# Layer 0 heads of a two-layer encoder kernel: attention weights turned by DMA transposes instead of on TensorE

## The reference, cut to what matters

```python
def stick_breaking_attention(q, k, v):      # strictly causal
        z = einsum(q, k) * scale
        log_stay = where(mask, log_sigmoid(-z), 0.0)
        after = cumsum(log_stay, reverse=True) - log_stay
        w = where(mask, exp(log_sigmoid(z) + after), 0.0)
        return einsum('bhqs,bshd->bqhd', w, vf)

def forgetting_attention(q, k, v, f_logit):  # causal
        logits = einsum(q, k) * scale + cq - cum_k
        p = softmax(where(mask, logits, -inf))
        return einsum('bhqs,bshd->bqhd', p, vf)
```

## Time and profile before

| | us |
|---|---|
| median of 3 runs (2885.72 to 2887.35) | 2886.86 |
| span of the profiled execution, first to last instruction | 2882.5 |
| sb pairs, from the first sb mask matmul to the first fox one | 240.9 (53.8 to 294.7) |
| fox pairs, to the end of the last pair's slots (about 521) | 226.3 |

### The profile page before, as it was taken

The page is one execution under the profiler, slowest core; times in us unless marked ns, Lnnn a source line. Parts: engine busy times, 40 slices in busy tenths (PEclk is TensorE's granted clock), DMA queues, the critical chain, the costliest instruction groups (busy, mean ns, idle before and its releaser), DMA issues.

```text
span 2882.5 us, 44624 instructions
## 1 busy us (share of the span) xinstructions
PE 2773.1 (96%) x16630; PEld 1456.3 (51%) x16912; DVE 1876.8 (65%) x2733; ACT 1081.0 (38%) x1765; POOL 1653.8 (57%) x918
## 2 busy tenths in 40 slices
PE   8999998899999999998899999999999999999998
PEld 4566665454444444444444444677764444444443
DVE  6777666486666674256999999677756756665042
ACT  4556555343333310014554333666653433332000
POOL 4777545336666669845347777600003566665884
PEclk9999999999999999999999999999999999999999
DMA  4222222431111143222113222211113211113322
GB/s 147 60 59 63 71 56 48 161 118 59 59 59 59 66 171 129 102 73 79 52 37 146 102 93 82 74 59 44 58 63 120 88 52 59 59 59 117 135 101 101
DMA packets 102990, 240.57 MB, mean 83 GB/s; under 512 B 42448, under 2 KB 42576, under 8 KB 102848
## 3 DMA queue, kind: packets, MB, share of 16 engines
q1 hardware_dynamic: 56352, 204.13, 19.9%
q10 hardware_dynamic: 46496, 34.48, 4.6%
HBM read 185.31 MB, written 31.51 MB: 75 GB/s over the span
## 4 chain that ended last, share of the span: by engine, by line
PE 85%; DVE 4%; ACT 3%; issue 3%; POOL 2%; ACTq 1%; DMA 0%; POOLq 0%; DVEq 0%
PE ps L1503 23%; PE ps L317 20%; PE ps L306 13%; PE ps L2310 6%; PE ps L584 5%; PE ps L341 3%; PE ps L2346 2%; PE ps L590 2%; PE ps L694 2%; PE ps L1830 2%; PE ps L779 2%; PE ps L756 2%; PE ps L2325 1%; PE ps L1874 1%; DVE pt_lo L715 1%
## 5 line engine op out<-in xcount | busy, mean ns | idle before, releaser
L262 POOL TENSOR_TENSOR w_hi<-w_stage,ones 128x1024 bf16<-128x1024 f32 (+1 forms) x115 | 235.1, 2044 | 137.9 <-PE ps L317 85.2
L265 POOL TENSOR_TENSOR w_lo<-w_stage,w_hi 128x1024 bf16<-128x1024 f32 (+1 forms) x115 | 262.6, 2283 | 9.0
L1320 DVE SCALAR_TENSOR_TENSOR x_res<-x_res,ps 128x1024 f32<-128x1024 f32 x32 | 39.0, 1218 | 338.1 <-PE ps L317 337.2
L317 PE MATMUL ps<-w_hi,hid_hi 128*128 128x512 bf16 x689 | 206.2, 379 | 1.6 <-POOL w_lo L265 0.8
L317 PE MATMUL ps<-w_lo,hid_hi 128*128 128x512 bf16 x690 | 206.4, 379 | 0.7
L317 PE MATMUL ps<-w_hi,hid_lo 128*128 128x512 bf16 x690 | 206.3, 379 | 0.7
L2310 PE MATMUL ps<-lat_hi,q_now 128*128 128x512 bf16 (+3 forms) x730 | 185.9, 323 | 1.2
L306 PE MATMUL ps<-xt_hi,w_hi 128*128 128x512 bf16 x598 | 179.2, 380 | 3.1 <-DVE score L1989 2.5
L306 PE MATMUL ps<-xt_hi,w_lo 128*128 128x512 bf16 x596 | 178.6, 380 | 0.8 <-issue 0.2
L306 PE MATMUL ps<-xt_lo,w_hi 128*128 128x512 bf16 x592 | 178.2, 381 | 0.8
L1503 PE MATMUL ps<-xt_lo,w_hi 128*128 128x512 bf16 x426 | 161.5, 379 | 0.5
(11 more groups left out here) (295 smaller groups left out, 7873.1 us busy)
## 6 DMA issues: line engine op xcount, KB each, us to landing
w_stage<-in_l_up SPq DMA_DIRECT2D x88, 512.0 KB, 3.2
w_stage<-in_l_down SPq DMA_DIRECT2D x88, 512.0 KB, 3.2
w_stage<-in_l_o SPq DMA_DIRECT2D x32, 512.0 KB, 4.7
w_stage<-in_l_q SPq DMA_DIRECT2D x32, 512.0 KB, 5.2
q_split<-q_out SPq DMA_DIRECT2D x32, 512.0 KB, 2.6
q_now<-q_split SPq DMA_DIRECT2D x16, 1024.0 KB, 4.8
w_stage<-in_l_qkv SPq DMA_DIRECT2D x24, 512.0 KB, 3.3
x_spilled<-x_res ACTq DMA_DIRECT2D x16, 512.0 KB, 2.6
```

Of the source, the lines that this page charges most:

```text
L262: pool.tensor_tensor(w_hi[slot][:, 0:cols], w_stage[slot][:, 0:cols], ones[:, 0:1].to_broadcast([P, cols]), ALU.mult).then_inc(w_cast[slot ...
L265: pool.tensor_tensor(w_lo[slot][:, 0:cols], w_stage[slot][:, 0:cols], w_hi[slot][:, 0:cols], ALU.subtract).then_inc(w_split[slot], 1)
L317: mm = pe.matmul(ps[:, bank + h, :], a[:, k, rows], w[slot][:, h * HALF:(h + 1) * HALF], start=(k == 0 and m == 0), stop=(k == tiles - 1 a ...
```

## The change

The transposes leave TensorE. ACT now writes the high half in the order in which the weights already lie (queries on partitions), SBUF to SBUF, one instruction for a step; DVE writes the low half in the same way. SP then issues a DMA transpose of the high half as soon as ACT has written it, and another of the low half when DVE has. Both halves are written in slot t+3 (`HI_AFTER = 0`), one slot earlier than before, so the values' matmuls keep their slots. PE waits for all eight transfers of a group before its first matmul. The `split` buffers share their bytes with `prob`, so what waited for PE's transposes (the fox exponentials, the sb scan) now waits for both transfers to land. POOL's result goes to `take` instead of `prob`; the setting of edge columns to zero ahead of the pairs goes away. SP's weight loads are written out between the transposes.

```diff
+        def weights_hi(act, kind, pair, t):
+            src, hi, _ = split_views(t)
...
+            act.activation(hi, src, ACT.Copy).then_inc(s_whi, 1)
+
+        def weights_lo(dve, pair, t):
+            src, hi, lo = split_views(t)
+            dve.wait_ge(s_whi, STEPS * pair + t + 1)
+            dve.tensor_tensor(lo, src, hi, ALU.subtract).then_inc(s_wlo0, 1)
+
+        def weights_turn(sp, pair, t):
+
+            m, g, qs = query_block(t) + 1, t % 8 // 4, query_block(t) % 4 * P
+            for part, (ready, done) in enumerate(((s_whi, s_turn_hi), (s_wlo0, s_turn))):
+                sp.wait_ge(ready, STEPS * pair + t + 1)
+                if t % 4 == 0 and part == 0:
+                    wait_if(sp, s_pv, 4 * pair + t // 4 - 1)
+                sp.dma_start_transpose(turned[g][:, 0:m, part, qs:qs + P],
+                                       split[t % 4][:, part, 0:m * P]).then_inc(done[t % 4], 16)
...
-                        pe.wait_ge(turning.lo, BATCHES * p + batches_through(4 * group + 3))
+                        for b in range(4):
+                            pe.wait_ge(s_turn_hi[b], turned_through(p, 4 * group + b))
+                            pe.wait_ge(s_turn[b], turned_through(p, 4 * group + b))
...
-                if kind_then == "sb":
-                    turning.turn(pe, p, t, s_wsb, STEPS * p + t + 1)
-                elif kind_then == "fox":
-                    turning.turn(pe, p, t, s_wfox, STEPS * (p - N_SB // 2) + t + 1)
...
-                    act.wait_ge(turning.made, turning.prob_free(pair, t))
+                    act.wait_ge(s_turn_hi[t % 4], turned_through(pair, t) - 16)
+                    act.wait_ge(s_turn[t % 4], turned_through(pair, t) - 16)
...
-                    wait_if(dve, turning.made, turning.prob_free(p1, t1))
+                    wait_if(dve, s_turn_hi[t1 % 4], turned_through(p1, t1) - 16)
+                    wait_if(dve, s_turn[t1 % 4], turned_through(p1, t1) - 16)
...
-            load_rest(sp, feed_qkv)
-            load_first(sp, feed_o0)
+            for n, pair in ((0, 1), (1, 1), (2, 1), (0, 2), (1, 2)):
+                load_piece(sp, feed_qkv, n, pair)
+            ahead = {4: (2, 2), 8: (0, 3), 13: (1, 3)}
+            for pair in range(N_PAIRS):
+                for t in range(STEPS):
+                    weights_turn(sp, pair, t)
```

More of the change, by code:

```diff
@@ L63 @@
 TURN_LAG = {"sb": 3, "fox": 3}
+HI_AFTER = 0
 assert SEQ % P == 0 and D_FF % P == 0 and N_DSA == 2 * N_PAIRS
@@ L524, in program, with weight_buffer @@
         stay = [low(f"stay{b}", [P, SEQ], F32) for b in range(2)]
-        prob = [low(f"prob{b}", [P, SEQ], F32) for b in range(2)]
+        def weight_buffer(place, b):
+            pair = sb(f"split{b}", [P, 2, SEQ], BF16, place.at)
+            return place(f"prob{b}", [P, SEQ], F32), pair
+        weights = [weight_buffer(low, b) for b in range(2)]
         assert low.at <= arena
@@ L529, in program @@
         mix_lo = room("mix_lo", [P, KT, SEQ], BF16)
-        prob += [room(f"prob{b}", [P, SEQ], F32) for b in range(2, 4)]
+        weights += [weight_buffer(room, b) for b in range(2, 4)]
+        prob, split = [w[0] for w in weights], [w[1] for w in weights]
         take += [room(f"take{b}", [P, SEQ], F32) for b in range(2, 4)]
@@ L674, in group_end @@
             return t % 8 // 4 if t % 4 == 3 else None
[L676 to L720, removed]
@@ L723, in program, with turned_through, split_views @@
-        turning = Turning("att0", prob, pt_hi, pt_lo, s_pv)
+        def turned_through(pair, t):
+            return 16 * (4 * pair + t // 4 + 1)
+        def split_views(t):
+            n = (query_block(t) + 1) * P
+            return take[t % 4][:, 0:n], split[t % 4][:, 0, 0:n], split[t % 4][:, 1, 0:n]
+        def weights_hi(act, kind, pair, t):
+            src, hi, _ = split_views(t)
+            if kind == "sb":
+                act.wait_ge(s_wsb, STEPS * pair + t + 1)
+            else:
+                act.wait_ge(s_wfox, STEPS * (pair - N_SB // 2) + t + 1)
+            act.activation(hi, src, ACT.Copy).then_inc(s_whi, 1)
@@ L777, in pair_tensor @@
                         ends = j == (TB, TB // 2)[g] - 1
-                        for m, pt in enumerate((pt_hi, pt_lo)):
-                            mm = pe.matmul(ps[:, 7, qs:512], v_both[hh][:, j, :], pt[g][:, j, qs:512],
+                        for m in range(2):
+                            mm = pe.matmul(ps[:, 7, qs:512], v_both[hh][:, j, :], turned[g][:, j, m, qs:512],
                                            start=(j == 0 and m == 0), stop=(ends and m == 1), skip_group_check=True)
@@ L992, in heads_sync @@
         def heads_sync(sp):
-            load_rest(sp, feed_qkv)
-            load_first(sp, feed_o0)
+            for n, pair in ((0, 1), (1, 1), (2, 1), (0, 2), (1, 2)):
[4 more added lines that the diff above has]
+                    weights_turn(sp, pair, t)
+                    n, further = ahead.get(t, (0, N_PAIRS))
+                    if pair + further < N_PAIRS:
+                        load_piece(sp, feed_qkv, n, pair + further)
+                    if (pair, t) == (N_PAIRS - 2, 8):
+                        load_piece(sp, feed_o0, 2, 0)
+                if pair == N_PAIRS - 3:
+                    for n in (3, 0, 1):
+                        load_piece(sp, feed_o0, n, 0)
         def heads_gpsimd(pool):
@@ L1057, in heads_vector @@
                 proj_evac_lo(dve, e, 0)
-            for b in range(4):
-                dve.memset(prob[b][:, P - 1:SEQ:P], 0.0).then_inc(s_edge, 1)
-            dve.wait_ge(s_edge, 4)
             all_pairs(dve, pair_vector)
```

35 lines of the change are left out of this document (18 added, 17 removed).

## The result

| | before, us | after, us |
|---|---|---|
| median of 4 runs | 2886.29 (2884.92 to 2887.35) | 2940.84 (2939.14 to 2944.53) |
| ratio, 95% interval | | 1.0186 [1.0172, 1.0201] |
| span of the profiled execution | 2882.5 | 2937.0 |
| sb part | 240.9 | 271.3 |
| fox part | 222.6 | 242.4 |

What follows compares the result with a forecast made beforehand. PE, busy 96% of the span, was taken to bound the kernel. Gains of 34 us (sb pairs) and 15 us (fox pairs) made 49 us off the 2882.5 us span: 2834, plus 4.4 for the median, 2838 us; range 2800 to 2920.

Steps and rivals of the forecast that it cites:

- the low half's price in "What the vector and scalar engines do now": Sb pairs: low half with both operands in SBUF takes 55 us instead of 47.9, bringing DVE to 189.6 us.
- Rival 4: Nothing much moves: DVE's SBUF reads meet POOL's, D about 5; kernel within 6 us of now; chance 0.07.
- Sb pairs, 207 us: Sb pairs: DVE's floor of 189.6 us plus 17.5 us gives 207 us, a gain of 34 us.
- a floor plus 17.5 us for uneven slots: Sb pairs: the bounding engine's idle time before, 17.5 us, was kept and added to DVE's floor of 189.6 us.
- The fox loop: Fox pairs: exponentials wait for transfers to land; two slots take 2.6 us + D, 6.6 us, so 211 us, gaining 15.
- D: Fox pairs: time from the low half's end to its landing, bounded by 2.4 to 5.6 us, taken as 4.0.
- rival 1: Fox pairs: short landings, D 3 us or less, gain 81 us, kernel 2806 us; chance 0.61 together with the forecast.
- SP's issue, 0.62 us: SP: 32 transposes and 3 loads a pair at 0.62 us each, 22 us a pair, hidden in 52.
- The queue: DMA queue: a pair's transposes at 31.6 ns a row take 36 us of some 52 us, so there is room.
- Rival 3: The DMA queue becomes the bound if transfers don't overlap: 86 us a pair, kernel 3111 us; chance 0.12.
- The removed transposes and the clock: Heads phase: removing 576 PE transposes cuts PE's busy time by 88.7 us; no clock change was forecast.
- Rival 2: Fox pairs: the loop decides with D above 5.6 us, slower, 2902 us at D = 6; chance 0.20.

Runs made afterwards that it cites:

- e6: Kernel before, PE's transposes kept, with the low half's float32 operand read from an SBUF constant instead of PSUM: 2978.9 us, ratio 1.0313.
- e9: Changed kernel with the low half's float32 operand read from unused PSUM banks: 2906.8 us, ratio 1.0069.
- e5: Changed kernel with POOL's splits of the coming pairs' weights cut to 16 columns: 2914.2 us, ratio 1.0094.
- e11: e8 with the low half's float32 operand read from PSUM: 2890.0 us, ratio 1.0008 to the kernel before.
- e1: Changed kernel with four buffers for the fox exponentials that share no bytes with `split`: 2933.4 us, ratio 1.0149.
- e12: e11 with both halves, the value matmuls and all that follows them a slot later: 2896.8 us, ratio 1.0024.
- e4: Changed kernel with only the high half's transposes issued, read by both matmuls: 2915.9 us, ratio 1.0090.
- e7: Changed kernel with plain DMA copies of the same rows in place of the transposes: 2929.7 us, ratio 1.0144.
- e8: e1 with one DMA transpose a step for both halves, 128 instructions: 2922.4 us, ratio 1.0114.
- e3: Changed kernel with DVE's low half cut to 16 columns: 2909.5 us, ratio 1.0068.

## Why the prediction was wrong, point by point

**The step that failed: the low half's price in "What the vector and scalar engines do now".** I took the row of 1.526 us for 1024 columns as the price of the form, 55 us, and kept scan and product as they were. It measured 80.5 us, and the scans, which the prediction left as they were, went from 108.2 to 122.4 (the same window's row of the kernel before for L896 has 108.22), and DVE's sum is 227.4 us, not 189.6. It isn't the form that costs more: low halves of 1024 columns took 1195 ns in the mean in the sb pairs, less than the 1526 of the row. At that price 288 blocks would be an estimated 43 us, so some 37 of the 80.5 are waiting. The cause is shown from four sides: the operand put into SBUF in the kernel before (e6), taken out of it in the changed one (e9), POOL's splits shortened (e5), and the timeline. Rival 4 names it ("its reads of SBUF meet POOL's"), with at most 6 us for the kernel, where it is 27.5 in the sb part alone.

The Trainium skill has the rule, and I left it out: SBUF — State Buffer, section "SBUF: two separate sides", says that a VectorE operation with two SBUF inputs and a GpSimd operation that reads SBUF take the same port as an exclusive lock, and that whichever starts second stands still until the first is through. The traces agree: the 640-column low half ended 0.68 us after POOL's split, the scans 2.1 ns a column after POOL's products, and 16 columns took 510 ns in the mean. The low half before the change read only one of its inputs from SBUF, and by the rule that leaves it alone: none took longer than 693 ns.

**Sb pairs, 207 us.** Measured 271.3. With the operand's cost taken away it is 244, so the larger part of this miss, 37 of 64 us, lies in a second step: a floor plus 17.5 us for uneven slots. PE's floor of 180.6 was itself too low (200.4 us busy in e11, at a clock of 0.96), and to the busiest engine there came 43.7 us of idle time and not 17.5. PE had 43 us less to do, and none of it showed. PE's waits moved to DVE's low halves of the projections, which share one PSUM bank (in e11 20.1 us for `nq_lo` and 10.6 for `nv_lo`, where the sb part before had 1.2 and none), and the copy in slot t+3 waits for POOL. Putting it later trades that for the landing. Which of these holds the 244 stays open: buffers of their own for the sb weights as well, which would tell the ring from the landing, weren't tried.

**The fox loop.** The wait was there (70.5 us of it), but it didn't set the pace. The landing was 2.9 us in the median, and up to 7.9. It is counted from the start of the issue: one low half ended at 346.38 us, its issue started at 346.4 and landed 2.9 us later, and the exponentials that waited for it started at 349.40. So the median D is that of rival 1 and not the 4.0 of the forecast, and the loop with it, 2.6 + 2.9 us for two slots, would give 176 us for the fox pairs: a gain, where there was a loss. Taking the wait out gave 8.1 us (e1). What together made 24.2 us (242.4 to 218.2) is the wait (8.1), SP's issues (2.3) and the SBUF operand (13.8) by the parts, in this order of removal; the totals of the same runs fell by 7.4, 11.0 and 32.4 us (the last with the sb part in it), so only the first of the three and their sum are firm. The forecast of 211 us to the end of the slots, some 207 as the fox part is counted here, wasn't reached even with all three gone and the copy a slot later (210.5 in e12).

**SP's issue, 0.62 us.** Measured 1.23 in the median, up to 4.2. It was hidden in the sb pairs (e4, e7), and worth at least 2 us in the fox pairs (e8).

**The queue.** Rival 3 was wrong: DMA's share was 0.63 to 0.70, not 1. At 31.6 ns a piece, the transposes' 36 us would be 54% of the 67.8 us that an sb pair took; the queue that carried them and the weight loads had 47.2% from 50 to 590 us.

**The removed transposes and the clock.** PE's busy time fell in the heads phase from 424.2 to 396.9 us by the earlier trace rows, 27 us and not 89: PE worked at a granted clock of 0.89 to 0.91, where before it was 0.99 to 1.00 (0.68 and 0.95 in the last pair). I hadn't counted that. It is a part of the difference only: at 0.96 in e11, PE was still busy 200.4 us in the sb part, 20 more than the forecast had.

**The sign.** Rival 2, slower by the fox loop with 2902 us, had the right side by luck: its condition, a landing above 5.6 us, held only for long ones, and that wait was worth 8 us. The time lies 21 us above the range.

## What to carry to other kernels

When work moves between engines, compare where each operand of the instructions that stay comes from, before and after: here a subtraction, with one operand moved from PSUM to SBUF, cost 27.5 us of the sb part beside a busy GpSimd, and 92 us of the kernel in e6. Price such an instruction from a row in which the neighbour engine runs as it will run, not from a row of the same form in another phase. And an engine that is busy 93% of a stage says little of what removing 43 us of its work gives, when the next engine is at 76% and the instructions wait in order: here it gave nothing, even with the operand's cost taken away.

## What the runs showed of the hardware

- 16-column VectorE subtractions with both operands in SBUF took 142 ns at least, 510 in the mean and 2035 at most in a phase with GpSimd busy (e3). GpSimd's product took 1684 ns in the mean before, 1840 beside VectorE's SBUF subtractions, and 1640 with its own splits cut (e5).
- In the changed kernel, VectorE scans that started behind a GpSimd product ended 1.61, 1.34 and 1.07 us after that product's end, for 767, 639 and 511 columns.
- The issue of a DMA transpose on SP took 1.1 to 4.2 us (median 1.23), of a plain copy of the same rows 0.49 to 3.4 (median 0.59); the landings differed by 0.3 us in the median.
- In e8 PE was busy all of the 9 us up to 375.0 us, then 2.14 of 4.8 us, the last 1.51 of them idle, and went on at half clock: the granted clock was 0.50 from 379.8 to 382.6 us and 1.00 from 382.8 on, which is 1.2 and 2.4 GHz; matmuls of 128 columns started 0.11 us apart and then 0.055.

```profile
379.80:382.60 2.80, 2.80 (x27) 2.80 (x28) 1.57 (x4) 1.89 (x4) 2.80 (x2) 0.50 1.11 252
382.80:385.30 2.50, 2.50 (x47) 2.48 (x45) 1.62 (x3) 1.01 (x3) 2.50 (x3) 1.00 1.32 176
```
